# Moving the fold of the compression's position weights into the first feed-forward

## The reference

```python
def compress(k, pos_emb, w1, w2):
    n_cmp = (k.shape[2] - CMP_BLOCK) // CMP_STRIDE + 1
    idx = jnp.arange(n_cmp)[:, None] * CMP_STRIDE + jnp.arange(CMP_BLOCK)[None, :]
    blocks = k[:, :, idx] + pos_emb
    flat = blocks.reshape(*blocks.shape[:3], CMP_BLOCK * HEAD_DIM)
    return jax.nn.gelu(flat @ w1) @ w2
```

## Time and profile before

| | |
|---|---|
| median of 3 runs | 1476.45 us |
| profiled execution | 1473.23 us |
| its span | 1471.5 us |
| mean granted clock of PE | 0.993 |
| PE busy | 1443.0 us (98%), 7240 matmuls |
| DVE busy | 937.9 us (64%) |
| ACT busy | 412.6 us (28%) |
| POOL busy | 95.1 us (6%), 75 instructions |
| DMA | 175.26 MB, mean 119 GB/s |

### The profile page before, as it was taken

How to read it: one execution, slowest core, us unless ns; L and a number is a source line. 1 busy time by engine, 2 the same in 40 slices (tenths; PEclk the granted TensorE clock), 3 DMA queues, 4 the chain that set the end, 5 groups by cost and what they waited for, 6 DMA issues and landing times.

```text
span 1471.5 us, 19415 instructions
## 1 busy us (share of the span) xinstructions
PE 1443.0 (98%) x7240; PEld 1172.0 (80%) x7240; DVE 937.9 (64%) x1666; ACT 412.6 (28%) x838; POOL 95.1 (6%) x75
## 2 busy tenths in 40 slices
PE   8999999999999999999999999999999999999997
PEld 7888777778888888888877777788887888888886
DVE  8787688976676665566666668765564444444443
ACT  6335355221111111013344556410122222221011
POOL 0000000200000001225200000000120000000110
PEclk9999999999999999999999999999999999999998
DMA  9344422446555564523221111133322222223332
GB/s 369 135 156 134 146 83 96 150 133 208 187 189 197 185 195 137 161 93 114 75 72 44 44 58 44 37 95 105 106 74 89 96 96 104 86 100 93 93 95 91
DMA packets 52464, 175.26 MB, mean 119 GB/s; under 512 B 5936, under 2 KB 6320, under 8 KB 52400
## 3 DMA queue, kind: packets, MB, share of 16 engines
q1 hardware_dynamic: 52400, 174.41, 35.2%
HBM read 172.29 MB, written 2.10 MB: 119 GB/s over the span
## 4 chain that ended last, share of the span: by engine, by line
PE 92%; DVE 5%; ACT 1%; issue 1%; DMA 0%; POOL 0%; SPq 0%; ACTq 0%; DVEq 0%
PE bank L664 20%; PE bank L665 20%; PE bank L666 20%; PE bank L1177 8%; PE bank L1197 2%; PE bank L1232 2%; PE bank L1208 2%; PE bank L1031 2%; PE bank L858 2%; PE bank L856 2%; PE bank L857 2%; PE bank L890 1%; PE bank L676 1%; DVE wl L1731 1%; PE bank L677 1%
## 5 line engine op out<-in xcount | busy, mean ns | idle before, releaser
L664 PE MATMUL bank<-uh,wh 128*128 128x512 f32 x808 | 316.6, 392 | 6.1 <-DVE wl L1731 4.6
L665 PE MATMUL bank<-ul,wh 128*128 128x512 f32 x808 | 315.8, 391 | 0.0
L666 PE MATMUL bank<-uh,wl 128*128 128x512 f32 x808 | 315.4, 390 | 0.0
L1729 DVE CAST wh<-wraw 128x1024 fp32r<-128x1024 f32 (+1 forms) x223 | 148.0, 664 | 194.0 <-PE bank L666 179.0
L1731 DVE TENSOR_TENSOR wl<-wraw,wh 128x1024 fp32r<-128x1024 f32 (+1 forms) x223 | 260.7, 1169 | 7.7
L664 PEld LDWEIGHTS bank<-uh,wh 128*128 128x128 f32 x808 | 152.3, 189 | 39.1 <-issue 5.8
L666 PEld LDWEIGHTS bank<-uh,wl 128*128 128x128 f32 x808 | 152.5, 189 | 31.9
L665 PEld LDWEIGHTS bank<-ul,wh 128*128 128x128 f32 x808 | 152.5, 189 | 31.5
L664 PE MATMUL bank<-hh,wh 128*128 128x512 f32 x352 | 137.5, 391 | 0.0
L666 PE MATMUL bank<-hh,wl 128*128 128x512 f32 x352 | 137.0, 389 | 0.0
L665 PE MATMUL bank<-hl,wh 128*128 128x512 f32 x352 | 137.0, 389 | 0.0
(11 more groups left out here) (360 smaller groups left out, 2253.9 us busy)
## 6 DMA issues: line engine op xcount, KB each, us to landing
ada<-in_w_ada_dram SPq DMA_DIRECT2D x94, 512.0 KB, 4.7
wraw<-in_w_in_dram SPq DMA_DIRECT2D x61, 512.0 KB, 3.4
wraw<-in_w_ffn_gate_dram SPq DMA_DIRECT2D x44, 512.0 KB, 3.4
wraw<-in_w_ffn_up_dram SPq DMA_DIRECT2D x44, 512.0 KB, 3.4
wraw<-in_w_ffn_down_dram SPq DMA_DIRECT2D x32, 512.0 KB, 3.4
wraw<-in_w_ffn_down_dram SPq DMA_DIRECT2D x16, 384.0 KB, 3.0
wraw<-in_w_out_dram SPq DMA_DIRECT2D x16, 256.0 KB, 2.7
wraw<-in_w_out_dram SPq DMA_DIRECT2D x8, 512.0 KB, 3.4
```

Source lines behind the costliest of these rows:

```text
L664: nc.tensor.matmul(bank[:], a, rh[:, k0 + k, :], start=(first and k == 0), stop=False)
L665: nc.tensor.matmul(bank[:], a, rl[:, k0 + k, :], start=False, stop=False)
L666: mm = nc.tensor.matmul(bank[:], b, rh[:, k0 + k, :], start=False, stop=(last and k == nk - 1))
L1729: V.tensor_copy(wh[:, slot, 0:n], wraw[:, slot, 0:n]).then_inc(w_hi, 1)
```

## The change

wpos and wfin move to the region at n_at, over tn and rstd. SP loads the same compression weights another time, straight into wpos: those of the keys behind iteration 6 of ff1, those of the values behind iteration 12, once the first five steps of c_pos are done. POOL folds them in place, in front of the square sums of norm 2. The later copy in w1c is still loaded for PE. DVE waits for the ten steps of c_pos before it writes tn in norm 2, and POOL waits for the compression's two bias matmuls (c_h) before it writes dm2, which lies over wfin.

```diff
-        wpos = at("wpos", [P, 16, P], where=s_at + 5 * K2)
-        wfin = at("wfin", [P, 2, P], where=s_at + 2 * K2 + 1024)
+        wpos = at("wpos", [P, 16, P], where=n_at + 4 * K2)
+        wfin = at("wfin", [P, 2, P], where=n_at + 3 * K2)
...
+            def pos_weights(n):
+
+                if n:
+                    sp.wait_ge(c_pos, 5)
+                else:
+                    sp.wait_ge(n_ul, 2 * KT)
+                w1 = t_in[("cmp_w1_k_2", "cmp_w1_v_2")[n]]
+                sp.dma_start(wpos[:], w1[0].rearrange("(j p) h -> p j h", p=P)).then_inc(c_pw, 16)
...
                     for i in range(ph.iters):
                         body(i)
+                        if name == "ff1" and i in (6, 12):
+                            pos_weights(i // 6 - 1)
...
             sum_squares(1)
-            for t in range(1, KT):
-                if t < KT - 1:
-                    add_square(2, t)
-                add_raw_square(t)
-
-            g.wait_ge(n_ul, KT * 3)
-            g.wait_ge(r_sum, 1)
-            g.wait_ge(c_in, 64)
+            g.wait_ge(vec_in, 32)
             for n, pos in enumerate((POS_K, POS_V)):
-                if n:
-                    g.wait_ge(c_pos, 5)
-                nc.gpsimd.tensor_tensor(wpos[:], w1c[:, n], vt2[:, pos:pos + 16].unsqueeze(2).broadcast_to([P, 16, P]),
+                g.wait_ge(c_pw, 16 * (n + 1))
+                nc.gpsimd.tensor_tensor(wpos[:], wpos[:], vt2[:, pos:pos + 16].unsqueeze(2).broadcast_to([P, 16, P]),
                                         ALU.mult).then_inc(c_pos, 1)
                 for level, k in enumerate((8, 4, 2, 1)):
                     g.wait_ge(c_pos, 5 * n + level + 1)
                     dst = wpos[:, 0:k] if k > 1 else wfin[:, n:n + 1]
                     nc.gpsimd.tensor_tensor(dst, wpos[:, 0:k], wpos[:, k:2 * k], ALU.add).then_inc(c_pos, 1)
+            for t in range(1, KT):
+                if t < KT - 1:
+                    add_square(2, t)
+                add_raw_square(t)
+
+            g.wait_ge(n_ul, KT * 3)
+            g.wait_ge(r_sum, 1)
...
+            g.wait_ge(c_h, 2)
             step2(nc.gpsimd.iota(dm2[:], [[8, T]], base=-8 * 384, channel_multiplier=-8,
...
                 v.wait_ge(n_rstd, nu)
+                if nu == 2:
+                    v.wait_ge(c_pos, 10)
```

More of the change, by code:

```diff
@@ L267, in build @@
         c_in, tab2, c_h, c_hb, c_hx, c_hg = (sem("c_in"), sem("tab2"), sem("c_h"), sem("c_hb"), sem("c_hx"), sem("c_hg"))
-        c_kv, c_kvc, c_pos = sem("c_kv"), sem("c_kvc"), sem("c_pos")
+        c_kv, c_kvc, c_pos, c_pw = sem("c_kv"), sem("c_kvc"), sem("c_pos"), sem("c_pw")
         c_z, c_v, c_e, c_t, c_wt = sem("c_z"), sem("c_v"), sem("c_e"), sem("c_t"), sem("c_wt")
@@ L605, in _ @@
             sum_squares(1)
+            g.wait_ge(vec_in, 32)
+            for n, pos in enumerate((POS_K, POS_V)):
+                g.wait_ge(c_pw, 16 * (n + 1))
+                nc.gpsimd.tensor_tensor(wpos[:], wpos[:], vt2[:, pos:pos + 16].unsqueeze(2).broadcast_to([P, 16, P]),
+                                        ALU.mult).then_inc(c_pos, 1)
+                for level, k in enumerate((8, 4, 2, 1)):
+                    g.wait_ge(c_pos, 5 * n + level + 1)
+                    dst = wpos[:, 0:k] if k > 1 else wfin[:, n:n + 1]
+                    nc.gpsimd.tensor_tensor(dst, wpos[:, 0:k], wpos[:, k:2 * k], ALU.add).then_inc(c_pos, 1)
             for t in range(1, KT):
@@ L612, in _ @@
             g.wait_ge(r_sum, 1)
-            g.wait_ge(c_in, 64)
-            for n, pos in enumerate((POS_K, POS_V)):
-                if n:
-                    g.wait_ge(c_pos, 5)
-                nc.gpsimd.tensor_tensor(wpos[:], w1c[:, n], vt2[:, pos:pos + 16].unsqueeze(2).broadcast_to([P, 16, P]),
[L618 to L622, removed]
             m = [0]
```

## The result

The changed kernel takes 1489.3 us (median of 5 runs, 1485.6 to 1490.44), the one before 1475.73 (5 runs beside it). The ratio, estimated from all the runs, is 1.0085, 95% interval 1.0073 to 1.0097: 12.5 us slower, with 10.8 to 14.3 possible (the two medians lie 13.6 apart). The forecast was 11.1 us and 1487.5. The profiled execution took 1489.3 with a span of 1486.9; that is 15.4 over the span before, whose execution lay 2.5 us under the 1475.73.

What follows compares the result with a forecast made beforehand. The prediction took TensorE (PE), 92% of the chain that ended last, to bound the kernel. Waits of 7.8 us plus clock loss of 3.3 gave +11.1 on 1476.45, about 1487.5 us, range 1477 to 1492.

Steps and rivals of the forecast that it cites:

- Folds out of the compression stage: Compression stage: PE never waited for the folds there, so moving them out saves PE 0.
- POOL's tables earlier, DVE's and POOL's new waits: Around norm 2 and compression: tables start near 676.9 and new waits are met early; 0, DVE's under 0.1 us.
- SP's new wait: SP's queue in ff1, before the second extra load: met over 40 us early; if late, all weight loads behind would be.
- The loads: SP's queue in ff1: two more 1 MB loads cost 0; the first lands at about 365.5.
- wpos's can start only then, some 1 us later than alone: First extra load in ff1: its bytes start when the up load's end, about 361.3, so it lands at about 365.5.
- start on time: Next weight load behind the extra load in ff1: issued 3.4 us later, after an issue of 0.84 us, so undelayed.
- rival C: ff1: the 1 MB transfers delay weight or modulation loads, the gate load landing over 3 us later than worked out; 1491, 8%.
- The hand-over: DVE and POOL in ff1: they take turns by whole instructions, delaying hl, cast and subtract; PE waits, sum 7.8 us.
- 3.9 each: PE's wait before up(6), and again six periods later: starts at 374.9, not 371.0, with the multiply starting at 365.6.
- The multiply's hold: Fold's multiply in ff1: keeps hl out for all 3.6 us; rows show such a hold only by 0.11 us.
- No second stall: ff1 after each PE wait: remaining adds, cast and subtract end near 378, before the gate unit due at 380.
- The clock: PE behind each wait in ff1: granted clock falls, 1.65 us each (between 0 and 2.4), 3.3 in all.
- Sum: Whole kernel: PE's waits and clock loss in ff1, 7.8 + 3.3 = +11.1 us.

Runs made afterwards that it cites:

- Experiment 5: Kernel before without POOL's ten fold and bias table instructions, the bias matmul using ones; ratio 0.999 (0.9979 to 1.0001) to the kernel before.
- experiment 7: Changed kernel with each fold cut into pieces of at most 2.3 us, one in each of five iterations, released by DVE's second modulation; 0.9989 of the kernel before.
- experiment 1: Kernel before plus the change's two extra 1 MB loads in ff1, used by nobody, folds where they were; ratio 0.9996 to the kernel before.
- experiment 9: Changed kernel with cut folds, plus small matmuls on PE in three gaps that the kernel before has too; ratio 0.9979, 1474.01 us beside 1476.65.
- experiment 3: Changed kernel with POOL's two multiplies alone, the eight adds left out and the bias matmul using ones; ratio 1.0038 to the kernel before, 5.6 us.
- experiment 6: Changed kernel with 13 small matmuls on PE between gate and up of iterations 6 and 12; ratio 1.0051 to the kernel before, 7.5 us.
- experiment 4: Changed kernel with the eight adds alone, the two multiplies left out; ratio 1.0034 to the kernel before, 5.0 us.
- experiment 8: Changed kernel, folds uncut, each also waiting for DVE's second modulation, 2.5 us before hl; ratio 1.0045 to the kernel before, 6.6 us.
- experiment 2: Changed kernel without its two extra loads, POOL setting wpos to ones and folding that; ratio 1.0091 to the kernel before.

## Why the prediction was right

- *Folds out of the compression stage: 0.* Right. Experiment 5 removes them altogether, with the stage at the same 63.2 us.
- *POOL's tables earlier, DVE's and POOL's new waits: 0.* Right as far as it shows: experiment 7 has them all and is not slower.
- *SP's new wait.* Right that it is long met in the changed kernel, and right in the warning that if it were late, the weight loads behind it would be: experiment 7 shows that.
- *The loads: 0.* Right in cost (experiment 1). Wrong in time: landing took 7.7 us, and the forecast had about 6.5 (359.0 to 365.5). The step that failed is "wpos's can start only then, some 1 us later than alone": the delay against w1c's 5.6 was 2.1. That the loads in front cause it fits experiments 7 and 9: there the second extra load was issued 6.5 us behind the up load, not 0.5, and landed after 5.6 and 5.7. Nor did the gate load behind it "start on time": its issue took 1.56 us and not 0.33, and it landed 6.9 us after its issue, at 371.3. It was needed 5.5 us behind the start of hf and came 3.5 behind it; the forecast had 2.5. So rival C was 2 us away, not 3. In the changed kernel the multiply began 1.65 and 1.43 us after hf started, not 0.1.
- *The hand-over.* Right, and it carried the late start too. The forecast gave 4.4 for a start after hl and 5.2 for the latest start in front of it; the first fold was of the one kind (wait 4.20), the second of the other (5.28). The term "3.9 each" was mis-sized through the start: 7.8 against 9.5.
- *The multiply's hold.* Right, 3.4 us (experiment 3). It was argued from 0.11 us in one row of before; the Trainium skill (SBUF — State Buffer, "SBUF: two separate sides"), by whose rule the lock is kept for the whole instruction, was the better witness, and now the trace agrees with it.
- *No second stall.* Right: from the subtract on, DVE is back in step within the period (hf waits 2.73 and 2.84 for PE).
- *The clock.* Right in kind, too small: 1.65 each forecast, 2.9 and 2.0 in the trace; experiment 6 got 3.1 back, at the first. The lower clock of the first fold lasted from before the wait's end to 383, where the forecast took the 1.7 us lost between 1108 and 1112 as its measure.
- *Sum.* 11.1 against 12.5 (10.8 to 14.3). The trace's own 15.4 holds 14.7 of the folds, less 1.6 for the fall that stayed away at 695, and 2.3 gathered before the folds, where nothing was changed (1.7 of it a clock fall at 237); both are what differs between two executions. That the sum came so near holds some luck: the two terms, forecast at 11.1, come to 14.4 in the trace, and the times show less because falls elsewhere in the program come in some executions and not in others.

## What to carry to other kernels

An engine's idle region is free for GpSimd work only if VectorE has room there too: look at VectorE's casts and two-input operations and at how much cover each has before TensorE wants its result, and compare it with the longest single GpSimd instruction. If the work must go there, cut it into pieces shorter than VectorE's gap and release each at the gap's start; moving it whole to the gap's start took off no more than half here. A load that waits in its queue for such a piece holds back every load behind it. A wait of TensorE costs more than its length when it brings the lower clock with it.

## What the runs showed of the hardware that was not expected

- The lower clock comes behind gaps of very different length, and not each time: behind the 1.57 us gap in front of qa2 in 4 of the 10 profiled executions without fillers there (before and experiments 1, 5 and 7), behind the 1.98 us gap at the start of ff1 in 6 of these 10, behind the 1.97 at the start of ff2 in 6, and behind neither the 2.18 nor the 2.49 of experiments 3 and 4. Behind the waits in ff1 of 3.03 and 3.05 (experiment 8), 4.19 (twice, experiment 2), 4.20 and 5.28 it fell each time. A fall costs 1.6 to 2.9 us.
- A 1 MB load in pieces of 0.5 KB landed after 5.6 us with a quiet queue and after 7.2 to 8.5 when issued right behind an up load. In that stretch of experiment 1 (355 to 375) the DMA engines moved 237 GB/s on average, and the gate load issued behind it landed after 7.6 us, not 3.4.
- GpSimd's wait for its turn is symmetric: in the first fold the last add of 128 columns took 1.32 us, against 0.46 undisturbed, since DVE's subtract was there first.
